# Prompt attention in steps of two heads, with turned probabilities normalised by a diagonal

## The reference, cut to what matters

```
rel   = relu(qi @ ki.T)                    # 4 index heads of 64, one key row
score = (wi * rel).sum(heads) * IDX_SCALE  # causal
idx   = top_k(score, 128)                  # per query
logits = (q @ k[idx].T) * HEAD_DIM ** -0.5 # 8 heads of 64, 2 key/value heads
p = softmax(logits);  o = p @ v[idx]
```

## Time and profile before

| | |
|---|---|
| median of 3 runs | 2845.17 us (2844.22 to 2848.72) |
| the profiled execution | 2842.32 us |
| its span, first to last instruction | 2840.5 us |
| TensorE / VectorE / ScalarE / GpSimd busy | 2731.1 / 950.6 / 817.4 / 1100.6 us |
| mean granted clock of TensorE | 0.983 |

### The profile page before, as it was taken

How to read it: one execution, slowest core, us unless ns; L and a number is a source line. 1 busy time by engine, 2 the same in 40 slices (tenths; PEclk the granted TensorE clock), 3 DMA queues, 4 the chain that set the end, 5 groups by cost and what they waited for, 6 DMA issues and landing times. The chain is left out here.

```text
span 2840.5 us, 53773 instructions
## 1 busy us (share of the span) xinstructions
PE 2731.1 (96%) x22316; PEld 2573.5 (91%) x22316; DVE 950.6 (33%) x2415; ACT 817.4 (29%) x1262; POOL 1100.6 (39%) x886
## 2 busy tenths in 40 slices
PE   5999999999989999999999999999998899999998
PEld 3999998999878889999989999989987779899998
DVE  3111113367584441111131111125657844411111
ACT  2321222222334233212233222232233332332221
POOL 4444444233212254444544344542332123544443
PEclk8999999999989999999999999999998999999999
DMA  6334346112212243333233343341122123322222
GB/s 234 134 119 147 129 153 224 68 46 88 79 35 77 94 161 134 119 128 144 77 129 125 134 149 128 118 162 60 48 90 67 30 90 126 113 94 90 100 78 86
DMA packets 104038, 312.99 MB, mean 110 GB/s; under 512 B 18140, under 2 KB 42106, under 8 KB 86410
## 3 DMA queue, kind: packets, MB, share of 16 engines
q1 hardware_dynamic: 96194, 290.87, 29.9%
q10 hardware_dynamic: 7640, 19.17, 1.8%
HBM read 299.56 MB, written 10.66 MB: 109 GB/s over the span
## 5 line engine op out<-in xcount | busy, mean ns | idle before, releaser
L920 POOL TENSOR_TENSOR w_lo<-raw,w_hi 128x512 fp32r<-128x512 f32 (+1 forms) x800 | 1008.4, 1291 | 1696.3 <-ACT w_hi L977 1696.3
L2014 PE MATMUL bank<-h_hi,w_hi 128*128 128x260 f32 x3744 | 1075.7, 287 | 2.4 <-ACT silu_g L1024 2.4
L2015 PE MATMUL bank<-h_hi,w_lo 128*128 128x260 f32 x3744 | 1059.6, 283 | 0.0
L2016 PE MATMUL bank<-h_lo,w_hi 128*128 128x260 f32 x3744 | 1059.2, 283 | 0.0
L2014 PEld LDWEIGHTS bank<-h_hi,w_hi 128*128 128x128 f32 x3744 | 709.7, 190 | 47.9 <-issue 46.5
L2015 PEld LDWEIGHTS bank<-h_hi,w_lo 128*128 128x128 f32 x3744 | 710.1, 190 | 0.0
L2016 PEld LDWEIGHTS bank<-h_lo,w_hi 128*128 128x128 f32 x3744 | 709.5, 190 | 0.0
L977 ACT CAST w_hi<-raw 128x2048 fp32r<-128x2048 f32 (+3 forms) x220 | 378.3, 1720 | 488.8 <-PE bank L2016 384.0
L2014 PE MATMUL bank<-mid_hi,w_hi 128*128 128x260 f32 x1232 | 351.5, 285 | 0.0
L2016 PE MATMUL bank<-mid_lo,w_hi 128*128 128x260 f32 x1232 | 348.4, 283 | 0.0
L2015 PE MATMUL bank<-mid_hi,w_lo 128*128 128x260 f32 x1232 | 348.3, 283 | 0.0
(11 more groups left out here) (327 smaller groups left out, 3443.8 us busy)
## 6 DMA issues: line engine op xcount, KB each, us to landing
raw<-in_w SPq DMA_DIRECT2D x120, 1024.0 KB, 4.8
raw<-in_w SPq DMA_DIRECT2D x64, 512.0 KB, 4.2
ada_ring<-in_ada SPq DMA_DIRECT2D x78, 320.0 KB, 5.2
raw<-in_w SPq DMA_DIRECT2D x32, 768.0 KB, 4.3
ada_ring<-in_ada SPq DMA_DIRECT2D x82, 256.0 KB, 4.9
raw<-in_w SPq DMA_DIRECT2D x32, 640.0 KB, 4.0
ada_ring<-in_ada SPq DMA_DIRECT2D x78, 192.0 KB, 5.1
out_y<-x ACTq DMA_DIRECT2D x4, 1040.0 KB, 9.3
```

The source lines that it names most:

```text
L920: last = pool.tensor_tensor(w_lo[j][:, cols], raw[j][:, cols], w_hi[j][:, cols].bitcast(F32), ALU.subtract)
L2014: mm(out, wh(wb), xh(xb), start=(n == 0), stop=False)
L2015: mm(out, wl(wb), xh(xb), start=False, stop=False)
L2016: last = mm(out, wh(wb), xl(xb), start=False, stop=(n == len(blocks) - 1))
```

## The change

The attention is one sequence of 16 steps, four per query tile; step (t, p) takes heads p and p + 4, which belong to the two key/value heads.

- *Logits*: both heads one after the other into banks 4 and 5; they are handed over with one semaphore. The query factor times the attention scale is multiplied into all query rows in `last_rows`, in two pieces with a signal each; `attn_ms`, the `neg_max` multiplication and the scale of the exponent go. VectorE negates the masked logits and keeps the running minimum, which is the exponent's bias.
- *Turning*: ScalarE writes diagonals of 1/sum (`diag`); TensorE multiplies the probabilities (stationary) with the diagonal (moving) in place of the transposes. Banks 6 and 7 take them. The scaling of `o_tok` goes.
- *Values*: once per two steps, 64 value columns stationary and turned probabilities moving, features of two heads in the two halves of the partitions, into a main bank. `o_tok` and its transposes go; high and low half are read from that bank, 8 times 256 columns.
- *Index*: heads in pairs, relu in place in banks 6 and 7, nothing for tile 0; tile 1's pairs lie between fills 0 and 1, those of tiles 2 and 3 in steps 0, 2, 4 and 6.
- Fills 4 to 27 go over 18 steps. `probs` and diagonals have four buffers, `probT` two with two heads each. SyncE's page loads wait for other signals.

```diff
+STEPS = 4 * TT
+STEP_FILLS, _at = [], 4
+for _n in (1, 1, 1, 2, 2, 1, 2, 1, 1, 2, 1, 2, 1, 1, 1, 1, 2, 1):
+    STEP_FILLS.append(range(_at, _at + _n))
+    _at += _n
...
+INDEX_AT = {0: (2, 0), 2: (2, 1), 4: (3, 0), 6: (3, 1)}
+INDEX_PAIRS = 2 * (TT - 1)
+TURNS = [min(s, 2 * 4) + 2 * max(0, s - 2 * 4) for s in range(STEPS + 1)]
...
-        rel = [area(f"rel{j}", [P, SEQ], 63712 + 2048 * j) for j in range(2)]
         score = area("score", [P, SEQ], 67808)
         work = area("work", [P, SEQ], 69856)
         mask = [area(f"mask{j}", [P, SEQ], 71904 + 2048 * j) for j in range(2)]
-        probs = [area(f"probs{j}", [P, SEQ], 76000 + 2048 * j) for j in range(2)]
-        probT = [area(f"probT{j}", [P, TT, P], at) for j, at in enumerate((80096, 84192, 86240, 88288))]
-        o_tok = area("o_tok", [P, NH, HD], 90336)
+        probs = [area(f"probs{j}", [P, SEQ], at) for j, at in enumerate((76000, 78048, 61152, 92544))]
...
+            return bank[6 + h % 2][:, 0:(t + 1) * P]
+        def turn_outs(s):
+            nk = (s // 4 + 1) * P
+            if 2 * nk <= SEQ:
+                return [bank[6][:, i * nk:(i + 1) * nk] for i in range(2)]
+            return [bank[6 + i][:, 0:nk] for i in range(2)]
+        def values_cols(k):
+            return slice(k % 2, 4, 2), slice(k // 2 * P, (k // 2 + 1) * P)
...
+            def exponents(l, step):
+                t, p = divmod(step, 4)
                 nk = (t + 1) * P
...
+                for i in range(2):
+                    h = p + 4 * i
+                    tile = probs[2 * (step % 2) + i]
+                    act.wait_ge(logits_taken, 2 * (STEPS * l + step) + i + 1)
+                    s.activation(tile[:, 0:nk], tile[:, 0:nk], ACT.Exp, scale=-1.0, bias=row_min[:, h:h + 1],
+                                 accum_out=row_sum[:, h:h + 1]).then_inc(probs_ready, 1)
+            def values(l, k):
+                unit = main_unit(l, "values", k)
+                wait_main(act, unit)
+                tiles, cols = values_cols(k)
+                s.copy(yc_hi[:, tiles, cols], bank[unit % 4][:, 0:2 * P].rearrange("p (c n) -> p c n", c=2))\
+                 .then_inc(y_hi_ready, 1)
+            def turned_probs(l, step):
+                nb = step // 4 + 1
+                if step >= 2:
+                    wait_main(act, main_unit(l, "values", step // 2 - 1))
+                dst = probT[step % 2]
+                if 2 * nb <= TT:
+                    act.wait_ge(turn_full, TURNS[STEPS] * l + TURNS[step + 1])
+                    s.copy(dst[:, :, 0:nb, :], bank[6][:, 0:2 * nb * P].rearrange("p (i b n) -> p i b n", i=2, b=nb))\
+                     .then_inc(turn_taken, 1)
+                    return
+                for i, src in enumerate(turn_outs(step)):
+                    act.wait_ge(turn_full, TURNS[STEPS] * l + TURNS[step] + i + 1)
+                    s.copy(dst[:, i, 0:nb, :], src.rearrange("p (b n) -> p b n", b=nb)).then_inc(turn_taken, 1)
+            def diagonals(l, step):
+                p = step % 4
+                act.wait_ge(inv_ready, STEPS * l + step + 1)
+                for i in range(2):
+                    h = p + 4 * i
+                    s.activation(diag[2 * (step % 2) + i][:], ident[:], ACT.Copy, scale=row_inv[:, h:h + 1])\
+                     .then_inc(diag_ready, 1)
+            def prompt_attention(l):
+                for step in range(STEPS + 2):
+                    if step in INDEX_AT:
+                        relus(l, *INDEX_AT[step])
+                    if step < STEPS:
+                        exponents(l, step)
+                    for i in STEP_FILLS[step]:
+                        fill(l, i)
+                    if values_at(step) is not None:
+                        values(l, values_at(step))
+                    if 1 <= step <= STEPS:
+                        turned_probs(l, step - 1)
+                    if step < STEPS:
+                        diagonals(l, step)
             def sample_fill(l, place):
                 for i in SAMPLE_FILLS[place]:
                     fill(l, i)
             def sample_attention(l):
...
+                wait_unit_taken(act, main_unit(l, "values", 2 * TT - 1))
                 for j in range(2):
...
                 ms = rot_ms[:, 3]
-                v.tensor_scalar(attn_ms[:, 0], ms[:, 0:TT, 0:NH], ATTN_SCALE, None, ALU.mult)
-                v.tensor_scalar(attn_ms[:, 1], ms[:, 0:TT, 0:NH], -ATTN_SCALE, None, ALU.mult)
                 v.tensor_tensor(ks, ks, bc(ms[:, :, 8:10].unsqueeze(3), [P, TT + 1, 2, HD]), ALU.mult)
                 v.tensor_tensor(ki, ki, bc(ms[:, :, 14:15].unsqueeze(3), [P, TT + 1, 1, HD]), ALU.mult)
-                qs = rot[0:NB, TT, 0:NH, :]
-                v.tensor_tensor(qs, qs, bc(ms[0:NB, TT, 0:NH].unsqueeze(2), [NB, NH, HD]), ALU.mult).then_inc(rotated, 1)
+                link(v.tensor_scalar(rot_ms[:, 2, :, 0:NH], ms[:, :, 0:NH], ATTN_SCALE, None, ALU.mult))
+                for tl in (slice(0, 2), slice(2, TT + 1)):
+                    qs = rot[:, tl, 0:NH, :]
+                    v.tensor_tensor(qs, qs, bc(rot_ms[:, 2, tl, 0:NH].unsqueeze(3), [P, tl.stop - tl.start, NH, HD]),
+                                    ALU.mult).then_inc(rotated, 1)
             def ya_tails(l):
...
                                            in1=causal[:, SEQ - nk:SEQ] if h == 0 else score[:, 0:nk],
...
+                                           op0=ALU.mult, op1=ALU.add).then_inc(index_taken, 1)
+                    dve.wait_ge(index_taken, use)
             def top_round(t, n):
...
+            def maxima(l, step):
+                t, p = divmod(step, 4)
                 nk = (t + 1) * P
...
+                dve.wait_ge(logits_full, STEPS * l + step + 1)
+                if step >= 2:
+                    dve.wait_ge(turn_full, TURNS[STEPS] * l + TURNS[step - 1])
+                for i in range(2):
+                    h = p + 4 * i
+                    v.tensor_tensor_reduce(out=probs[2 * (step % 2) + i][:, 0:nk], in0=bank[4 + i][:, 0:nk],
+                                           in1=mask[t % 2][:, 0:nk], scale=-1.0, scalar=-TAKEN, op0=ALU.add,
+                                           op1=ALU.min, accum_out=row_min[:, h:h + 1]).then_inc(logits_taken, 1)
+            def values_tail(l, k):
+                unit = main_unit(l, "values", k)
+                tiles, cols = values_cols(k)
+                dve.wait_ge(y_hi_ready, Y_HEADS * l + 7 + k + 1)
+                v.tensor_tensor(yc_lo[:, tiles, cols], bank[unit % 4][:, 0:2 * P].rearrange("p (c n) -> p c n", c=2),
+                                yc_hi[:, tiles, cols].bitcast(F32), ALU.subtract).then_inc(main_taken[unit % 4], 1)
+            def prompt_attention(l):
+                for step in range(STEPS + 3):
+                    t, p = divmod(step, 4)
+                    rounds = range(4 * p, 4 * p + 4) if t + 1 < TT else range(0)
+                    if step < STEPS:
+                        maxima(l, step)
+                    for n in rounds:
+                        top_round(t + 1, n)
+                        if n % 4 == 0 and step in INDEX_AT:
+                            scores_of(l, *INDEX_AT[step])
+                    if step < STEPS:
+                        dve.wait_ge(probs_ready, 2 * (STEPS * l + step + 1))
+                        v.reciprocal(row_inv[:, p:NH:4], row_sum[:, p:NH:4]).then_inc(inv_ready, 1)
+                    if values_at(step - 1) is not None:
+                        values_tail(l, values_at(step - 1))
+                    if p == 3 and t + 1 < TT:
+                        make_mask(t + 1)
+                    if step < STEPS + 2:
+                        for i in STEP_FILLS[step]:
                             fill(l, i)
...
+            def low_banks(l, turns, pairs):
+                if turns:
+                    pe.wait_ge(turn_taken, TURNS[STEPS] * l + turns)
+                if pairs:
+                    pe.wait_ge(index_taken, 2 * (INDEX_PAIRS * l + pairs))
...
+            def logits(l, step):
+                t, p = divmod(step, 4)
                 nk = (t + 1) * P
...
+                if step > 0:
+                    pe.wait_ge(logits_taken, 2 * (STEPS * l + step))
+                for i in range(2):
+                    rows = slice(i * HD, (i + 1) * HD)
+                    last = mm(bank[4 + i][:, 0:nk], rotT[rows, p, t * P:(t + 1) * P], rotT[rows, 4, 0:nk],
+                              start=True, stop=True)
+                last.then_inc(logits_full, 1)
+            def turn_probs(l, step):
+                nb = step // 4 + 1
+                pe.wait_ge(diag_ready, 2 * (STEPS * l + step + 1))
+                low_banks(l, TURNS[step], 2 + sum(at <= step + 1 for at in INDEX_AT))
+                for i, out in enumerate(turn_outs(step)):
+                    for kb in range(nb):
+                        ks = slice(kb * P, (kb + 1) * P)
+                        last = mm(out[:, ks], probs[2 * (step % 2) + i][:, ks], diag[2 * (step % 2) + i][:],
```

(28 more changed lines are left out.)

249 lines of the change are left out of this document (82 added, 167 removed).

## The result

| | before | after |
|---|---|---|
| median | 2845.40 us (4 runs) | 2795.34 us (4 runs, 2791.91 to 2800.08) |
| ratio | | 0.9823, 95% interval 0.9809 to 0.9837 |
| the profiled execution | 2842.32 us | 2792.26 us |
| its span; mean granted clock | 2840.5 us; 0.983 | 2790.4 us; 0.989 |

What follows compares the result with a forecast made beforehand. TensorE, busy 2731 of 2840.5 us, was taken as the bound. Stages falling from 170.1 to 142 and 174.6 to 145 us, less 1.0 lost outside, gave 56.6 us: 2789 us from 2845.2, range 2762 to 2825.

Steps and rivals of the forecast that it cites:

- Logits pair: Prompt attention, TensorE: logits of two heads in different row halves take one visit, near 1.2 us at 512 keys.
- turn records: Prompt attention, TensorE: records of the products turning probabilities by a diagonal start 0.11 us apart.
- value visit: Prompt attention, TensorE: value products of four heads at four key blocks take near 1.8 us.
- no queue of column halves: Value products in two output column halves overlap; the rival that they queue: 2803 us, chance 0.1.
- 2x and not 4x for the diagonal: Turning a block costs 0.222 us instead of 0.11; the rival of four times a transpose: 2819 us, chance 0.03.
- Sum by tile: Layer 0's attention, head and four tiles, the later of TensorE and VectorE in each: 129 us before added waits.
- VectorE's share: Sign of being right: VectorE over 90% busy in tiles 1 and 2 of the prompt attention.
- Waits: Attention stage: 5 us for value banks meeting q fills, 2 for uneven fills; tile 2 VectorE 32.4 against TensorE 28.9.
- Clock: Attention tiles of layer 0: 12 us of full clock lacking before, half kept as a loss, 6 us.
- Rival 4: Attention stages keep today's low clock and waits, 20 us a layer: 149 and 153 us, total 2803 us, chance 0.25.
- Rival 3: Steps with rounds: late diagonals from ScalarE make the trip serial, 43 us a layer, total 2875 us, chance 0.07.
- Outside the attention: Query scaling in `last_rows` delays the first signal 0.5 us a layer, 1.0 us in all; other moved work hides.

Runs made afterwards that it cites:

- e7: Kernel before with only queries scaled ahead, negated logits and running minimum, without the negated-maximum multiplication: 2842.4 us, ratio 0.9961 to 1.0002.
- e12: Changed kernel, but in step 11 VectorE combines the q fill's results after the second top-8 round instead of the fourth: 2796.0 us.
- e4: Changed kernel, but behind each of 64 minima VectorE waits for it and multiplies one 128x1 column nobody needs: 2824.1 us.

## Why the prediction was right, and where its steps were off

- *Prices of TensorE.* Logits pair 1.13 us (put down: near 1.2), turn records 0.11 apart, value visit 1.97 (near 1.8), no queue of column halves, 2x and not 4x for the diagonal. All right. What a change of tiling mode costs by itself no run shows. The Trainium skill ("TensorE: Matmul & The Clock Gate", section "Terms") calls the transpose mode 4x faster for FP32; the turns of 1.95 and 1.04 us say 1.9x with the start in it. By that page 2819 us, by the rows 2789, measured 2795.
- *Sum by tile.* Forecast, then layer 0: 13 and 14.8, 20.8 and 22.3, 27.7 and 28.4, 32.4 and 37.2, 35.5 and 42.2 us. TensorE's busy time in tiles 0 and 1 was met (20.8 and 27.7), and the head is 13.3 us in layer 1, where the clock stayed up; in the last stretch TensorE's busy time is 39.8 instead of 35.5. That term was mis-sized mostly by the lag of the steps: the turn of step 11 (1.50 us) and the value visit of tile 2 (1.53) fall behind the first logits of tile 3, and I had left them in tile 2, where VectorE would have covered them.
- *VectorE's share.* I had named over 90% busy in tiles 1 and 2 as a sign of being right. It is 89% and 85% (25.2 of 28.4, 31.8 of 37.2 us); most of its idle time in tile 2 is the wait for TensorE's slow visits behind step 11. The share is 93% in tile 0.
- *Waits.* I had put 5 us for value visits meeting q fills in steps 11 to 15, three times 1.6, behind VectorE's low half. TensorE's wait for VectorE there is 6.8 us, but 5.6 of it stand in step 11 behind VectorE's rounds. Place right, mechanism wrong; sized well by luck. Waits, VectorE's surplus and idle time together are 9.9 us in layer 1 (143.3 less 133.4 busy), where the sum had 5 + 2 + 3.5.
- *Clock.* Forecast 6 us left of 12 in layer 0; the time not granted within the stage is 5.1 there, from 11.9, and 3.4 in layer 1, from 15.4. The two stages together gain 18.8 us, nearly all of the 19.4 that the profiled execution gains in granted clock (49.1 to 29.7). In the means over all executions it is 16.1 (51.0 to 34.9), so about a third of the 50 us is clock. I put that down to TensorE no longer standing between single heads; no run shows it by itself, but in e7, which keeps single heads, 25.6 us are not granted in the stages, nearly as much as the 27.3 before. Keeping half was right for layer 0 and too little trust for layer 1 (145 forecast, 143.3 measured). Rival 4, waits and clock as before, is refuted by the same figures.
- *Rival 3*, the serial trip: TensorE doesn't wait for diagonals; ScalarE waits 13.0 us for the reciprocals, three us at the longest, under cover of a fill. The diagonals themselves take 397 ns and 11.1 us a layer, against the estimate of 7; the larger price is hidden too.
- *Outside the stage.* Forecast 1.0 us lost. With the ends as in the table of runs the stages gain 23.2 and 29.6 us, 52.8 together, and the span 50.1: 2.7 us lost. 2.3 us are lost ahead of layer 0's stage: 1.1 stood already at 600 us, before anything that the change touches, 0.1 to 0.2 came with the scaling of the queries, for which I had 0.5, and 1.0 because the first pair of index products waits 2.6 us for VectorE where it waited 1.6. 1.9 us are won between the stages and 2.4 lost behind layer 1's; that goes with the clock, of which 3.4 us less are not granted in the former stretch and 4.5 us more in the latter. And 1.8 us a layer, which those ends count to the stage, are given back behind the tail, where the copies collide with GpSimd. I had named no price for that: GpSimd's subtractions had come to stand beside the copies, and what they ran into was not asked.
- *The sum* was 56.6 us, the median gave 50.1. By the stage table, whose end lies ahead of the copies, the stages gave 25.2 and 31.3, 56.5 together, against 28 and 29.6 forecast; so 6.4 us were lost outside it where I had 1.0. That the stages came out near the forecast is partly luck: the mis-sized last stretch and tile 2 were paid from the 13 us set aside for waits and clock. The miss of the total lies outside: 2.3 us ahead of layer 0's stage, 3.5 behind the two stages, and the rest goes with the clock of these executions.

## What to carry to other kernels

When a pipeline is recast in steps, write the sum by what stands between two marks in the queue, with the lag of each stage in it, and ask of every value that an engine returns late what longer work stands ahead of it in that engine's queue. Order products that write different output halves, or read different row halves, so that neighbours differ. Put no small VectorE operation beside a GpSimd subtraction if something waits for it. Judge edits of a few us by the median of several executions, and look at the work and at the clock apart, the clock over all executions: one trace of e12 had 15 us more not granted where the mean of five had 4.

## What the runs showed of the hardware that was not expected

- Overlap of two 64-column products needs them near each other in the order: 16 products (32 records) in 1.97 us alternating, 2.57 in runs of four, 3.33 in runs of eight.
- Small VectorE operations are held up by GpSimd's subtractions of 128x512: two copies of 64x32 or 64x16 take 2.33 or 2.47 us beside them and 0.35 to 0.38 without, and seven of 32 operations of one column in e4 take 0.42 to 0.90 us instead of 0.16. Minima, which read a bank, take the same 0.69 us at 512 keys with and without.
- A dependent operation of one column, with the waits before and behind it, costs VectorE 0.31 us of pace in tile 2 for a busy time of 0.16.
- The same idle time of 2.1 us at the same place is followed by 3.4 us not granted in layer 0 of the changed kernel (clock 0.91, then 0.52 in the stretches shown), by none in its layer 1, and by 5.1 in layer 0 of e12 (0.79, then 0.50).
